# Three changes of order in a fused transformer kernel: a table load on ScalarE, Fourier gating on VectorE, stick-breaking scores on TensorE

## What is computed

```python
def stick_breaking_attention(q, k, v):        # per block of 128 queries
    z = jnp.einsum('bhqd,bhkd->bhqk', qb, k).astype(jnp.float32) * scale
    log_keep = jnp.where(past, jax.nn.log_sigmoid(-z), 0.0)
    log_later = lax.cumsum(log_keep, axis=3, reverse=True) - log_keep
    a = jnp.where(past, jnp.exp(log_beta + log_later), 0.0)
...
def _even_mix(h, w_in, a_conv_w, a_conv_b, a_ln_g, a_ln_b, a_pw_w, a_pw_b, b_fw, w_out):
    a_val, a_glu, a_gate, b_val, b_gate = _split(h @ w_in, [A_WIDTH, A_WIDTH, A_WIDTH, B_WIDTH, B_WIDTH])
    u = a_val * jax.nn.sigmoid(a_glu)
    u = jax.nn.silu(_layernorm(_dwconv(u, a_conv_w) + a_conv_b, a_ln_g, a_ln_b))
    y_a = (u @ a_pw_w + a_pw_b) * jax.nn.silu(a_gate)
    y_b = _fourier_mix(b_val, b_fw) * jax.nn.silu(b_gate)
    return jnp.concatenate([y_a, y_b], axis=-1) @ w_out
```

## Time and profile before

| | |
|---|---|
| runs | 749.2, 747.08, 745.29 us |
| median | 747.08 us |
| profiled execution | 744.48 us, of which the span of the profile 742.7 us |
| granted clock of TensorE | 0.994 |
| busy: PE, PEld | 725.7 us (98%), 665.2 us |
| busy: DVE, ACT, POOL | 640.5 us (86%), 393.1 us (53%), 8.3 us |
| chain that ended last | PE 79%, DVE 9%, DMA 5%, ACT 3%, issue 2% |
| three products of the linear layers (L1607, h) | 386.3 + 382.6 + 382.5 us, overlapping |
| modulations with `cond` (L905) | 88 instructions, 1220 ns each |
| remainders of the weights (L940) | 82 instructions, 2288 ns each |
| table loads on ACT | 12, 1283 ns each |

### The profile page before, as it was taken

The page is one execution under the profiler, slowest core; times in us unless marked ns, Lnnn a source line. Parts: engine busy times, 40 slices in busy tenths (PEclk is TensorE's granted clock), DMA queues, the critical chain, the costliest instruction groups (busy, mean ns, idle before and its releaser), DMA issues.

```text
span 742.7 us, 12665 instructions
## 1 busy us (share of the span) xinstructions
PE 725.7 (98%) x5202; PEld 665.2 (90%) x5202; DVE 640.5 (86%) x1082; ACT 393.1 (53%) x532; POOL 8.3 (1%) x18
## 2 busy tenths in 40 slices
PE   8899999999999999999999999999989999999996
PEld 4789989999989999999999998888768899999995
DVE  5777898897998899999988999999899979888653
ACT  4254366668356555554557555345462345555742
POOL 0000000000000000000000000000000000000000
PEclk9999999999999999999999999999999999999998
DMA  9989999866664676666656176877405642675101
GB/s 367 420 323 395 388 395 355 315 245 216 220 227 170 221 255 253 236 227 235 248 199 227 57 248 157 219 206 192 113 23 227 226 144 83 221 275 187 58 1 57
DMA packets 24875, 163.98 MB, mean 221 GB/s; under 512 B 2758, under 2 KB 4591, under 8 KB 5360
## 3 DMA queue, kind: packets, MB, share of 16 engines
q1 hardware_dynamic: 21404, 150.37, 54.2%
q0 software_dynamic: 1152, 8.39, 5.6%
q10 hardware_dynamic: 2262, 4.42, 1.8%
HBM read 153.71 MB, written 1.07 MB: 208 GB/s over the span
## 4 chain that ended last, share of the span: by engine, by line
PE 79%; DVE 9%; DMA 5%; ACT 3%; issue 2%; DVEq 0%; ACTq 0%; SPq 0%
PE psum L1607 67%; DVE w_lo L905 4%; DMA raw<-in_w 4%; PE psum L1698 3%; DVE w_lo L940 2%; DMA arena<-in_w 2%; ACT w_hi L415 1%; PE psum L2102 1%; PE psum L2126 1%; PE psum L2114 1%; PE psum L1789 1%; PE psum L1646 1%; PE psum L1771 1%; PE psum L1675 1%; DVE xs L1415 0%
## 5 line engine op out<-in xcount | busy, mean ns | idle before, releaser
L1607 PE MATMUL psum<-h_hi,w_hi 128*128 128x256 f32 (+1 forms) x1280 | 386.3, 302 | 3.5 <-DVE h_lo L1381 2.2
L1607 PE MATMUL psum<-h_lo,w_hi 128*128 128x256 f32 (+1 forms) x1280 | 382.6, 299 | 0.0
L1607 PE MATMUL psum<-h_hi,w_lo 128*128 128x256 f32 (+1 forms) x1280 | 382.5, 299 | 0.0
L1607 PEld LDWEIGHTS psum<-h_hi,w_hi 128*128 128x128 f32 x1280 | 244.6, 191 | 13.8 <-issue 4.1
L1607 PEld LDWEIGHTS psum<-h_lo,w_hi 128*128 128x128 f32 x1280 | 244.7, 191 | 7.9 <-issue 0.2
L1607 PEld LDWEIGHTS psum<-h_hi,w_lo 128*128 128x128 f32 x1280 | 244.6, 191 | 7.5
L940 DVE TENSOR_TENSOR w_lo<-raw,w_hi 128x2048 fp32r<-128x2048 f32 x82 | 187.6, 2288 | 26.1 <-ACT w_hi L415 25.2
L415 ACT CAST w_hi<-raw 128x2048 fp32r<-128x2048 f32 x90 | 171.3, 1906 | 38.9 <-DMA raw<-in_w 29.8
L905 DVE SCALAR_TENSOR_TENSOR w_lo<-raw,cond 128x1024 fp32r<-128x1024 f32 x88 | 104.2, 1220 | 0.8
L905 DVE SCALAR_TENSOR_TENSOR w_lo<-raw,arena 128x1024 fp32r<-128x1024 f32 x48 | 56.8, 1220 | 11.4 <-DMA raw<-in_w 5.8
L638 ACT ACTIVATE arena<-psum,vec 128x256 f32<-128x256 f32 x44 | 22.5, 564 | 58.6 <-DVE g_lo L1182 54.2
(11 more groups left out here) (246 smaller groups left out, 710.0 us busy)
## 6 DMA issues: line engine op xcount, KB each, us to landing
raw<-in_w SPq DMA_DIRECT2D x138, 1024.0 KB, 4.9
w_lo<-raw POOLq DMA_DIRECT2D x8, 1024.0 KB, 7.2
arena<-in_w SPq DMA_DIRECT2D x3, 1024.0 KB, 14.6
xs<-in_xs SPq DMA_DIRECT2D x1, 1024.0 KB, 9.0
consts<-diff ACTq DMA_DIRECT2D x4, 256.0 KB, 9.2
cond<-diff ACTq DMA_DIRECT2D x1, 1024.0 KB, 8.6
xs<-in_xs ACTq DMA_DIRECT2D x1, 1024.0 KB, 7.5
out<-xs SPq DMA_DIRECT2D x2, 384.0 KB, 2.5
```

Source lines behind the costliest of these rows:

```text
L1607: last = mm(out, w[a], x[b], start=start and n == 0, stop=stop and n == 2, skip_group_check=skip)
```

## The change

Three edits of order; no operation of the computation is added or dropped.

1. On ACT the load of the logarithm and exponential table moves from ahead of the four squares of the layer norm to behind them.
2. On DVE the gatings of the Fourier groups 2 and 3 move from behind the pointwise tiles 2 and 3 into the loop of the normalisation, behind its steps 3 and 5. The modulation chunk ahead of LIN_EOUT + 1, which was done in two parts, one ahead of the pointwise tiles and one behind the last remainders, is done in one piece at the place of the second.
3. On the PE the stick-breaking scores of the first pair stand ahead of its transposes instead of behind them. For the other pairs nothing changes.

```diff
--- before.py
+++ after.py
@@ -745,12 +745,12 @@
                         act.wait_ge(sem("glu_done"), 4)
                     ins = nc.scalar.activation(sgate[:, t:t + 2, :], src, ACT.Silu)
                 ins.then_inc(sem("ein_evac"), 1)
-            load_ln_exp()
             for t in range(4):
                 act.wait_ge(sem("centered"), t + 1)
                 nc.scalar.activation(ln_tmp[:, t, :], conv[:, t, :], ACT.Square).then_inc(sem("ln_squares"), 1)
                 if t < 2:
                     fourier_evac(t + 2)
+            load_ln_exp()
             act.wait_ge(sem("ln_sum"), 2)
@@ -1380,11 +1380,10 @@
-                if t == 1:
-                    fourier_gated(1)
+                if t in (1, 3, 5):
+                    fourier_gated((t + 1) // 2)
 
             (m,) = mods_before(LIN_EOUT + 1)
-            mod_static(m, LIN_EOUT + 1, part=0)
             for pair in ((0, 1), (2,), (3,)):
@@ -1396,8 +1395,6 @@
                                                        by_parity(sgate[:, t, :], parity), ALU.add, ALU.mult
                                                        ).then_inc(sem("y_a"), 1)
-                    if t >= 2:
-                        fourier_gated(t)
                 for t in pair:
@@ -1406,7 +1403,7 @@
                 dve.wait_ge(sem("y_hi"), 5 + t)
                 nc.vector.tensor_tensor(h_lo[:, t, :], y_b[:, t, :], h_hi[:, t, :].bitcast(F32),
                                         ALU.subtract).then_inc(sem("y_lo"), 1)
-            mod_static(m, LIN_EOUT + 1, part=1)
+            mod_static(m, LIN_EOUT + 1)
             split(LIN_PW + 2, done=1)
@@ -1804,10 +1801,12 @@
                 else:
                     if h == 1:
                         pe.wait_ge(sem("proj_evac"), LIN_GATE)
-                    transposed_probs(p)
                     if p:
+                        transposed_probs(p)
                         weighted_values(p - 1, 1)
                     stick_scores(p)
+                    if p == 0:
+                        transposed_probs(p)
                 if h:
                     pe.wait_ge(sem("gate_evac"), h)
```

## The result

| | before | after |
|---|---|---|
| median of 20 runs each | 745.16 us (743.61 to 749.72) | 748.58 us (746.72 to 750.35) |
| ratio after/before | | 1.0036, 95% interval 1.0024 to 1.0047 |
| profiled execution, of which the span | 744.48, 742.7 us | 747.04, 745.2 us |
| granted clock | 0.994 | 0.997 |

The changed kernel is slower by 2.7 us (1.8 to 3.5). The forecast was +0.9 us. The predicted median of 748.0 came close to 748.58 by two errors that largely cancel: it started from the 747.08 of three runs, 1.9 us above the median that twenty runs gave, and its difference was 1.8 us too small (the ratio, which compares runs side by side, says 2.7; the two medians lie 3.4 apart).

What follows compares the result with a forecast made beforehand. DVE's saturated queue from 554.3 to 590 us (35.29 of 35.70 busy) feeds a nearly gapless PE; +2.42 - 0.74 - 0.8 = +0.9 us on the 747.08 median gives 748.0, no measurable change. Range 745.2 to 750.2 us.

Steps and rivals of the forecast that it cites:

- Part 1: First transposes of the attention: scores fill the PE's 1.11 us wait, pair 1 takes some back, -0.8 us.
- Rival B: Scores' gain doesn't arrive, through pair 1's probabilities or a DMA-paced cast: +1.7 us, 748.8; chance 0.12.
- Part 2: Table load runs hidden behind the squares, the second sum's wait goes, pointwise projection starts 0.49 us earlier.
- -0.74: Last pointwise remainder, with gating gone, at 552.94 instead of 553.68 us; the load's 0.49 is inside.
- Rival D: Squares need their own table, so a load precedes them again: at most 0.5 us lost, 748.5; chance 0.04.
- Part 3: Extra modulation half enters DVE's full stretch: +2.42 less 0.74, +1.68 us, wait at squares 0.89 to 2.85.
- Rival A: The extra modulation half is hidden, the PE keeps all gains: -1.5 us, 745.5; chance 0.14.
- rival C: TensorE's clock falls in the lengthened wait at 589.6 to 592.5 us: 1.3 us more, 749.3; chance 0.13.

Runs made afterwards that it cites:

- experiment 12: Changed kernel plus zero products on the PE in both waits, 12 at the squares and 10 ahead of the pointwise projection: 1.0010 against the kernel before, +0.7 us.
- 8: Changed kernel with the third output chunk's evacuation moved ahead of the second modulation for the next layer: 1.0028 against the kernel before, +2.1 us.
- experiment 5: Kernel before with only the table load moved behind the squares: 0.9982 against the kernel before, -1.3 us.
- 9: Kernel before plus 10 zero products on the PE in its 2.2 us wait ahead of the pointwise projection: 1.0000 against the kernel before, 0.0 us.
- experiment 1: Changed kernel with the modulation kept in its two old halves and places: 0.9970 against the kernel before, -2.2 us.
- experiment 3: Kernel before with only the modulation put in one piece behind the remainders: 1.0052 against the kernel before, +3.9 us.
- 4: Kernel before with only the first pair's stick scores ahead of its transposes: 0.9990 against the kernel before, -0.7 us.
- 6: Kernel before with only the gatings of groups 2 and 3 moved into the normalisation loop: 0.9993 against the kernel before, -0.5 us.
- 10: Kernel of experiment 1 with four final scalings moved into DVE's gaps at the last two pointwise tiles: 0.9968 against the kernel before, -2.4 us.
- 2: Changed kernel plus 12 zero products on the PE between the squares of tiles 3 and 4: 1.0005 against the kernel before, +0.4 us.
- 11: Kernel of 10 plus the 10 zero products of 9 ahead of the pointwise projection: 0.9966 against the kernel before, -2.5 us.

## Why the prediction was right and wrong

**Part 1, the scores (-0.8 taken).** Right in its mechanism. In the trace of the changed kernel DVE's probabilities for pair 0 end at 103.34 us and the gate projection starts at 104.14, 0.80 behind; before, the same distance was 1.99 us. That is 1.19 us gained at the place, and part goes back at pair 1, as predicted. What is left at the first mark: the nine traces with the edit start the 300 products between 170.88 and 173.25 us, mean 171.75; the five without between 171.95 and 173.58, mean 172.48. The difference is -0.73 us, with about 0.4 of uncertainty from that scatter. Rival B, a cast paced by a transfer, shows in two of the nine. It is to be seen in experiment 12, in the timelines of ACT and, below it, of the PE:

```profile
112.14 1.90 ACT L415 CAST w_hi<-raw 128x2048 fp32r<-128x2048 f32 x1 [5.33 <-DMA raw<-in_w]
113.94 0.58 ACT L593 COPY arena<-psum 128x512 f32<-128x512 f32 x1
```
```profile
114.58 0.39 PE L1604 MATMUL psum<-h_hi,w_hi 128*128 128x256 f32 x1 [1.79 <-ACT arena L593]
```

The gate's copy stands behind a cast whose weights came late, and the PE waits 1.79 us for it. So in these traces B was a matter of single executions (8 and 12), not of the kernel.

**Part 2, the table load (-0.49 inside -0.74).** Right in its mechanism, too small in size. The load runs at 531.63 (predicted 532), hidden by 0.92 us, and the second sum's wait is gone. The timelines of the PE, of the kernel before and of the changed one, show what that is worth:

```profile
527.09 1.02 PE L1987 MATMUL psum<-arena,c 128*128 128x512 f32 x2
...
533.84 1.12 PE L1993 MATMUL psum<-arena,c 128*128 128x512 f32 x2 [0.49 <-DVE arena L1349]
```
```profile
526.67 1.02 PE L1986 MATMUL psum<-arena,c 128*128 128x512 f32 x2
...
529.32 3.62 PE L1944 MATMUL psum<-consts,att 128*128 128x256 f32 x16
532.77 1.02 PE L1992 MATMUL psum<-arena,c 128*128 128x512 f32 x2
...
539.49 0.47 PE L1604 MATMUL psum<-h_hi,w_hi 128*128 128x512 f32 x1 [2.24 <-DVE h_lo L1381]
```

From the first sum to the second are 6.75 us before and 6.10 after. The prediction took the end of the row of Fourier products as the earliest start of the sum; in fact the sum starts 0.17 us ahead of that end (529.32 + 3.62 = 532.94), as matmuls overlap. The logarithm then starts 1.06 us behind the sum's start (at 533.83), before it was 1.16 (at 535.00). So the pointwise projection starts 12.82 us behind the first sum instead of 13.57 (540.66): 0.75 us, and the other traces with and without this edit agree to 0.02. In time, experiment 5 puts it at -1.3 (-2.3 to -0.4). The page "ScalarE: Activation LUTs", section "What ACT_TABLE_LOAD costs", of the Trainium skill puts a switch at about 2.66 us with its drain; the rows here show no drain. The next load starts at 535.20 and the operation behind it at 536.49, 1.29 us later, like the 1.30 us of the earlier trace rows. Around the moved load it can't be read, as the 2.20 us to the next operation end with a wait for the PE. Rival D is out: no further load stands ahead of the squares.

**Part 3, the half in the full stretch (+1.68 net).** Right in place and nearly in size. The split came at 560.15 instead of 559.10, +1.05 us. Of what the attention had gained 0.42 is left at 516 us (515.94 against 516.36 in the chain); with that taken off, the split is later by 1.47 us. The second half of the piece is in it with 2.40 us, and the stage ahead of it gained 0.93 instead of the 0.74 of the sum, as part 2 was worth more. Experiments 9 and 12 give +1.50, and the balance of the two traces +1.56. Next to experiment 1 the half costs less, 2.02 us: with all gatings ahead of it DVE is done with it at 545.81 us there, when the first pointwise tile has long been ready (5.14 us behind the start of the projection in the changed kernel, which is 544.4 in experiment 1). So it no longer fills idle time alone. The wait at the squares is 2.70 (predicted 2.85), the idle time of DVE ahead of the first pointwise tile 0.78 (0.7), the wait at the last remainder 0.3 (0.3), the one at the second chunk 0.31 (0.5). Rival A, the hidden half, is out by experiment 3.

**The step that failed** is the case against rival C. It said that the clock stayed at 1.00 after the 2.2 us wait at 538.4, and on that row the clock was left out of the sum and C got 0.13. The row was right, and said less than I read from it. In other executions of the same stretch the clock did fall: at the wait of 2.2 us near 540 in six of the eleven traces without products in it (3, 4, 5, 6, 8, 10), at the wait of 2.6 to 2.7 us near 590 in two of three (the changed kernel and 8, not 3). Near 540 the PE has the same instructions in all of these kernels, and the mean clocks of the runs of one kernel differ as well. Whether it falls is a matter of the execution, and one trace shows one draw. The right reading was a term with a chance: a wait that grows from 0.9 us to this length buys a fall in a good part of the executions; by the mean clocks, in most. The price that C named, 1.3 us, was near the 1.50 of the row. C's total, 0.9 + 1.3 = +2.2, lies inside the measured interval of 1.8 to 3.5, the forecast's +0.9 does not. Experiments 2 and 12 show the cause: with the PE kept busy in that wait, the changed kernel stands at +0.4 and +0.7, next to the sum of +0.9 that leaves the clock out.

"TensorE: Matmul & The Clock Gate" of the Trainium skill, Part 1, which says that an idle PE falls to half its clock, was named beside C. The traces agree with it in 8 of 14 such waits, and so it deserved more than one row against it.

**What stays open.** The products took 2.0 to 2.3 us out of the medians, and one fall costs 1.50 us in the trace. With intervals of about 1 us on each, this is no contradiction; whether a second effect of a few tenths is in it, the runs can't say. The share of executions with a fall is an estimate from mean clocks, and for the rounds of the main result those of the kernel before are not on record.

## What to carry to other kernels

In a stretch where an engine is busy without a hole, count what enters it at full length and look for the wait at its end; splitting work so that half of it fills an idle hole was worth 3.9 us here (2.6 to 5.2), more than the half's own 2.4. A row of matmuls overlaps with the next, so what follows can start a little before the row's printed end; that was 0.17 us here. Where an edit lengthens a TensorE wait from under 1 us to over 2, add the price of slow products behind it with a chance, and don't rule it out by one trace in which the clock stayed up: look at the same wait in several. If such a wait can't be removed, products of zeros in it are a cheap way to see what the clock is worth.

## What the runs showed of the hardware that was not expected

- The clock of TensorE after a wait differs between executions in which it does the same work up to there. Near 540 us, after 2.2 us without a product, the granted clock fell to 0.50 in 6 of 11 traces. After 2.6 to 2.7 us near 590 it fell in 2 of 3. After the 0.9 us waits at the squares it was never seen to fall, nor in any of five waits that held products of zeros (2, 9, 11, and both of 12). Elsewhere it is as mixed: near 22 us, behind a wait of 1.3 to 2.0 us for a transfer, it fell in 9 of the 14 traces; a wait of 2.38 us at 104 us in experiment 3, and one of 1.79 in 12, had no fall behind them.
- The fall shows behind the wait here, not in it: in the changed kernel the window of 590 to 592 us has 1.00, the next ones 0.87, 0.50 and 0.78. The 48 products behind it take 7.24 us instead of 5.74.
